# Two heads side by side in the products with values, exponentials after the copies of transposes, and the norms' small products in four groups of the TensorE array

## What is computed

```python
def rms_norm(x, g):
    y = xf * lax.rsqrt(jnp.mean(xf * xf, axis=-1, keepdims=True) + EPS)
    return (y * g.astype(jnp.float32)).astype(x.dtype)

# neighbourhood attention: local keys with a bias, and context keys
s = jnp.concatenate([s_loc + bias, s_ctx], axis=-1)
p = jax.nn.softmax(s, axis=-1)
a = p_loc @ v_loc + p_ctx @ v_ctx            # 8 heads of 64

# multi-head latent attention
q = rms_norm(cq) @ w_uq ; kn = rms_norm(rms_norm(ckv) @ w_uk)
s = qn @ kn + rope(qr) @ rope(kr)            # 64 + 32 features a head
m = softmax(s * QK_DIM ** -0.5) @ v          # 8 heads of 64

# PEER: rows of two tables of 16384 x 1024 are gathered per token
act = gelu(einsum('thkd,td->thk', exp_u[idx], hb))
out = einsum('thk,thkd->td', gate * act, exp_v[idx])
```

## Time and profile before

| what | value |
|---|---|
| median of three runs | 5595.64 us (5584.25 to 5604.5) |
| the profiled execution, its own time | 5615.22 us |
| its span, first to last instruction | 5613.4 us |
| PE busy | 4447.6 us, 79% |
| DVE busy | 3051.5 us, 54% |
| POOL busy | 2763.0 us, 49% |
| ACT busy | 1241.3 us, 22% |
| mean granted TensorE clock | 0.867 of full speed |

### The profile page before, as it was taken

The page is one execution under the profiler, slowest core; times in us unless marked ns, Lnnn a source line. Parts: engine busy times, 40 slices in busy tenths (PEclk is TensorE's granted clock), DMA queues, the critical chain, the costliest instruction groups (busy, mean ns, idle before and its releaser), DMA issues.

```text
span 5613.4 us, 57357 instructions
## 1 busy us (share of the span) xinstructions
PE 4447.6 (79%) x19168; PEld 2455.9 (44%) x19168; DVE 3051.5 (54%) x8176; ACT 1241.3 (22%) x3643; POOL 2763.0 (49%) x2566
## 2 busy tenths in 40 slices
PE   7989798889997887997855558999788889655555
PEld 4467643433585344653411115558533455311111
DVE  0211767776217776556676542431677655777643
ACT  1321222333212321112211112540133211111111
POOL 0000466666304655666677770000366466777776
PEclk9889898888998888998977888999888999877778
DMA  5544799988747878999999992114688799999999
GB/s 189 189 153 142 282 367 340 335 311 331 253 137 279 324 286 304 379 398 358 356 390 369 394 389 83 55 39 154 221 310 318 278 366 399 391 391 391 362 403 353
DMA packets 464130, 1651.73 MB, mean 294 GB/s; under 512 B 51168, under 2 KB 57440, under 8 KB 463840
## 3 DMA queue, kind: packets, MB, share of 16 engines
q0 software_dynamic: 368640, 1342.34, 63.2%
q1 hardware_dynamic: 95200, 305.73, 15.2%
HBM read 1645.77 MB, written 2.10 MB: 294 GB/s over the span
## 4 chain that ended last, share of the span: by engine, by line
PE 50%; POOL 15%; DVE 13%; DMA 11%; issue 7%; ACT 3%; SPq 0%; DVEq 0%; POOLq 0%; ACTq 0%; PEldq 0%
PE banks L647 16%; PE banks L925 10%; DMA vb<-in_peer_v_dram,idx 8%; POOL vb L1446 8%; POOL ub L1435 7%; DVE ub L1386 5%; PE banks L736 4%; PE banks L663 3%; PE banks L773 3%; PE banks L835 3%; PE banks L812 2%; PE banks L758 2%; PE banks L823 1%; DMA ub<-in_peer_u_dram,idx 1%; PE banks L715 1%
## 5 line engine op out<-in xcount | busy, mean ns | idle before, releaser
L1435 POOL DMA_INDIRECT ub<-in_peer_u_dram,idx x1280 | 1424.1, 1113 | 2270.7 <-DVE idx L1374 1375.1
L925 PE MATMUL banks<-vb,dg 128*64 128x512 f32 x5120 | 1571.7, 741 | 695.7 <-DMA vb<-in_peer_v_dram,idx 626.4
L1386 DVE CUSTOM_DVE_ANT_0 ub<-ub,h2cur 128x1024 f32<-128x1024 f32 x1280 | 1529.6, 1223 | 611.1 <-DMA ub<-in_peer_u_dram,idx 485.9
L1446 POOL DMA_INDIRECT vb<-in_peer_v_dram,idx x1280 | 1338.3, 1046 | 561.0 <-issue 342.5
L925 PEld LDWEIGHTS banks<-vb,dg 128*64 128x64 f32 x5120 | 406.7, 160 | 1596.1 <-issue 1336.4
L647 PE MATMUL banks<-region,wring 128*128 128x256 f32 x3840 | 882.2, 390 | 35.8 <-ACT region L989 25.3
L647 PEld LDWEIGHTS banks<-region,wring 128*128 128x128 f32 x3840 | 738.7, 195 | 215.8 <-issue 104.9
L1135 ACT ACTIVATE dg<-consts,wgt 128x64 f32<-128x64 f32 x1280 | 358.4, 337 | 836.5 <-PE banks L925 425.3
L647 PE MATMUL banks<-h2T,wring 128*128 128x256 f32 x1280 | 316.9, 406 | 21.1 <-ACT h2T L989 21.1
L1329 DVE SCALAR_TENSOR_TENSOR region<-region,banks 128x256 f32<-128x256 f32 x120 | 50.5, 421 | 486.0 <-PE banks L647 485.9
L736 PE MATMUL banks<-region,wring 128*128 128x256 f32 (+1 forms) x1056 | 260.7, 404 | 48.0 <-ACT region L989 48.0
(11 more groups left out here) (146 smaller groups left out, 4004.9 us busy)
## 6 DMA issues: line engine op xcount, KB each, us to landing
wring<-w_gate_dram SPq DMA_DIRECT2D x120, 512.0 KB, 5.0
wring<-w_mod_dram SPq DMA_DIRECT2D x96, 512.0 KB, 4.6
wring<-w_pq_dram SPq DMA_DIRECT2D x80, 512.0 KB, 5.4
wring<-w_branch_dram SPq DMA_DIRECT2D x60, 512.0 KB, 3.6
wring<-w_out_dram SPq DMA_DIRECT2D x40, 512.0 KB, 4.7
ub<-in_peer_u_dram,idx POOLq DMA_INDIRECT x1280, 6.6
vb<-in_peer_v_dram,idx POOLq DMA_INDIRECT x1280, 6.6
region<-in_na_rpb_dram SPq DMA_DIRECT2D x64, 256.0 KB, 3.0
```

The lines of the kernel that those rows point to most:

```text
L925: ins = nc.tensor.matmul(bank(ACC[a])[64 * g:64 * g + 64, :], dg[:, n % DG_RING, :], vb[:, n % V_RING, a * 512:(a + 1) * 512], start=first ...
L1386: nc.vector.tensor_tensor_reduce(out=ub[:, n % U_RING, :], in0=ub[:, n % U_RING, :], in1=h2cur[:, g, :], scale=1.0, scalar=0.0, op0=ALU.mu ...
L1435: pool.indirect_dma_start(ub[:, n % U_RING, :], None, u_rows, bass.IndirectOffsetOnAxis(ap=idx[:, u % IDX_RING, j:j + 1], axis=0)).then_in ...
L1446: pool.indirect_dma_start(vb[:, n % V_RING, :], None, v_rows, bass.IndirectOffsetOnAxis(ap=idx[:, u % IDX_RING, j:j + 1], axis=0)).then_in ...
```

## The change

1. `mixv` works on two units at a time: the products of units i and i+1 alternate, one in columns 0 to 63 of the array and one in columns 64 to 127, into one bank; ACT copies both with one instruction of 128 partitions.
2. On ACT the exponentials are a step of their own (`exp`), behind the copies of the transposes. They read the bank always: the biased scores are now written back into their bank by DVE, and that bank is emptied by the exponential, not by DVE. `pr` has two buffers instead of three and `ptr` three instead of two.
3. `stat` is issued for four items together. Item i uses column group i mod 4 of 32 columns; `rs` has 128 rows, and the spread of an item contracts the 32 rows of its group. `sq` has 8 buffers.

```diff
@@ run_batch @@
+            done = 0
             for i, it in enumerate(items):
...
+                if it["key"][2:] == ("cq", 1):
+                    it["group"] = items[i - 1]["group"]
+                else:
+                    it["group"] = i % 4
                 emit(("raw", l, name, i), cost)
-                if i:
-                    emit(("stat", l, name, i - 1))
-            emit(("stat", l, name, len(items) - 1))
+                if i - done == 4:
+                    emit(("stat", l, name, done, i))
+                    done = i
+            emit(("stat", l, name, done, len(items)))
@@ run_units @@
-                if 3 <= i:
-                    emit(("mixv", l, s, kind, i - 3))
+                if i < n:
+                    emit(("exp", l, s, kind, i))
+                if i >= 4 and i % 2 == 0:
+                    emit(("mixv", l, s, kind, i - 4))
@@ PE, stat @@
+                    for i in range(i0, i1):
+                        it, g = items[i], groups[i]
+                        which, q0, q1 = it["pick"][0]
+                        off = which - it["row"]
+                        ins = nc.tensor.matmul(bank(cnt["held"])[32 * g:32 * g + 32, 0:N], sel[q0:q1, off:off + 32],
+                                               sq[q0:q1, i % 8, :], start=(i == groups.index(g)),
+                                               stop=(g not in groups[i + 1:]), tile_position=(q0, 32 * g), skip_group_check=True)
@@ PE, spread @@
+                    g0 = 32 * it["group"]
                     for p0, p1, row in it["spread"]:
-                        ins = nc.tensor.matmul(bk[p0:p1, 0:N], ident[0:32, row:row + 1].broadcast_to([32, p1 - p0]),
-                                               rs[0:32, :], start=True, stop=True, tile_position=(0, p0))
+                        ins = nc.tensor.matmul(bk[p0:p1, 0:N], ident[g0:g0 + 32, g0 + row:g0 + row + 1].broadcast_to([32, p1 - p0]),
+                                               rs[g0:g0 + 32, :], start=True, stop=True, tile_position=(g0, p0))
@@ PE, mixv @@
-                    for j, vv in enumerate(un["v"]):
-                        ins = nc.tensor.matmul(bk[un["po"]:un["po"] + 64, 0:P], vv, ptr[:, i % 2, j * P:(j + 1) * P],
-                                               start=(j == 0), stop=(j == nv - 1))
+                    for j in range(nv):
+                        for e, un in enumerate(two):
+                            ins = nc.tensor.matmul(bk[64 * e:64 * e + 64, 0:P], un["v"][j],
+                                                   ptr[:, (i + e) % 3, j * P:(j + 1) * P],
+                                                   start=(j == 0), stop=(j == nv - 1), tile_position=(0, 64 * e),
+                                                   skip_group_check=True)
@@ DVE, biased score @@
-                        frees(nc.vector.tensor_tensor_reduce(out=pr[:, i % 3, 0:512], in0=bk, in1=bias[:, nb % 2, :], scale=-1.0,
...
-                        emptied(dve, key)
-                        dve.sem_inc(neg_max, 1)
+                        nc.vector.tensor_tensor_reduce(out=bk, in0=bk, in1=bias[:, nb % 2, :], scale=-1.0, scalar=st[:, 0:1],
+                                                       op0=ALU.add, op1=ALU.min, accum_out=st[:, 2:3]).then_inc(neg_max, 1)
```

More of the change, by code:

```diff
@@ L434, in na_stage @@
                         un = dict(key=(l, s, "na", t, h), q=naq[s][rows, ch, t * P:(t + 1) * P], po=p0,
-                                  dest=aT[s][rows, ch, t * P:(t + 1) * P], bias=None)
+                                  dest=aT[s][:, ch, t * P:(t + 1) * P], bias=None)
                         if s:
@@ L750, in _ @@
                 elif op == "stat":
-                    _, l, name, i = step
+                    _, l, name, i0, i1 = step
                     items = batches[(l, name)]
-                    it = items[i]
-                    cnt["sq"] += 1
+                    groups = [it["group"] for it in items]
+                    cnt["sq"] += i1 - i0
                     pe.wait_ge(sq_ready, cnt["sq"])
-                    which, q0, q1 = it["pick"][0]
-                    off = which - it["row"]
-                    ins = nc.tensor.matmul(bank(cnt["held"])[0:32, 0:N], sel[q0:q1, off:off + 32],
-                                           sq[q0:q1, i % 3, :], start=(i == 0), stop=(i == len(items) - 1),
-                                           skip_group_check=True)
-                    if i == len(items) - 1:
+                    for i in range(i0, i1):
[5 more added lines that the diff above has]
+                                               stop=(g not in groups[i + 1:]), tile_position=(q0, 32 * g), skip_group_check=True)
+                    if i1 == len(items):
                         fills(ins, (l, name, "stat"))
@@ L1007, in _ @@
                     last_spread[0] = batches[(l, name)][-1]["key"] + ("spread",)
-                    frees(nc.scalar.activation(rs[0:32, :], bk[0:32, 0:N], ACT.Sqrt, bias=epsc[0:32, 0:1]), key)
+                    rows = 32 * (max(it["group"] for it in batches[(l, name)]) + 1)
+                    frees(nc.scalar.activation(rs[0:rows, :], bk[0:rows, 0:N], ACT.Sqrt, bias=epsc[0:rows, 0:1]), key)
                 elif op == "values":
@@ L1035, in _ @@
                     st = stats[:, i % 4, :]
-                    if i >= 3:
-                        whole(act, t_hist[-1])
                     off = 0
                     for a, (_, w) in enumerate(un["k"]):
-                        dst = pr[:, i % 3, off:off + w]
                         key = un["key"] + ("s", a)
-                        if a == 0 and un["bias"] is not None:
-                            nc.scalar.activation(dst, dst, ACT.Exp, bias=st[:, 2:3], scale=-1.0, accum_out=st[:, 4:5])
-                        else:
-                            bk = whole(act, key)
-                            ins = nc.scalar.activation(dst, bk[:, 0:w], ACT.Exp, bias=st[:, 2:3], accum_out=st[:, 4 + a:5 + a])
-                            frees(ins, key)
+                        bk = whole(act, key)
+                        sign = -1.0 if a == 0 and un["bias"] is not None else 1.0
+                        frees(nc.scalar.activation(pr[:, i % 2, off:off + w], bk[:, 0:w], ACT.Exp, bias=st[:, 2:3], scale=sign,
+                                                   accum_out=st[:, 4 + a:5 + a]), key)
                         off += w
@@ L1237, in _ @@
                     emptied(dve, (l, name, "stat"))
-                    link(nc.vector.reciprocal(rs[0:32, :], rs[0:32, :]))
+                    rows = 32 * (max(it["group"] for it in batches[(l, name)]) + 1)
+                    link(nc.vector.reciprocal(rs[0:rows, :], rs[0:rows, :]))
                     dve.sem_inc(rs_ready, 1)
```

47 lines of the change are left out of this document (17 added, 30 removed).

## The result

The changed kernel takes 5535.24 us (median of 4 runs, 5523.83 to 5558.92), the kernel before, run beside it, 5600.07 us (5584.25 to 5610.14). The ratio is 0.9884, 95% interval 0.9855 to 0.9913: 65 us faster. The forecast was 148 us, so 83 us of it did not come.

What follows compares the result with a forecast made beforehand. PE bounds stretches without background; with background DMA sets the pace, in `mla_stage` PE partly too. Savings of 73 us without and 75 with background make 148 us: median 5595.6 to 5448 us, range 5370 to 5540.

Steps and rivals of the forecast that it cites:

- A pair of units: Products with values: two column groups run at once, 24 instructions cost what 12 did, 0.73 us PE work saved per unit.
- A period of two units: PE-bound `na_stage`: two units take some 6.8 us instead of 7.49, with about 0.6 us wait in every second unit.
- The 0.21 us per item: Norms' stats: cost by the skill's smaller factor instead of 0.16 us, making the sum about 8 us smaller over 210 items.
- keys of mla: Norms of mla's keys: ACT becomes the bound at 0.73 us per item, so only 0.38 us is saved.
- The spreads of eleven keys: Spreads of mla's keys: four row groups overlap, DVE takes an item in 0.43 us instead of 0.87, saving 0.43 us each.
- the 73 us forecast without background: Stages without background: CTX 29 us, norms of B 5, `na_stage` 11 and `mla_stage` of A 28 in the second layer.
- The first: Attention with background: a 2.5 us sum between most units covers the bank wait, so 0.73 us is all PE work saved.
- Norms of A and B and `na_stage`: First layer, 658 to 1185 us: PE saves 37 us, but DMA sets the pace; a quarter, 9 us, is saved.
- The last rival: Slower, by the held bank: PE waits for the whole chain every unit, 3.2 us over 96 units, 5755 us; chance 0.06.
- The second: Three `mla_stage`s with background: 60% of 34 to 35 us PE saving each, taken as 20, 22 and 22 us.
- The background keeps its pace: Rival: gathers' latency sets stages with background; only others gain, 56 us without row-group overlap, 5540 us; chance 0.16 with clock.
- Its kin, the clock: Rival: clock in emptier stages falls from 0.87 to 0.80, taking back most of 75 us; chance 0.16 shared with background.

Runs made afterwards that it cites:

- with one group: Changed kernel with all items in one column group: stats still four together but one behind the other, spreads in one row group; 5816.67 us, 0.9984 of the kernel before.
- norms alone: Kernel before with only the change's stats and spreads, attention as before; 5763.95 us (0.9896), again 5778.14 (0.99), on the chip of four kernels 5791.94 (0.9936).
- pairs in turn: Changed kernel with the two units of a pair one behind the other instead of side by side; 5580.51 us, 0.9963 of the kernel before.
- the change with late background: Changed kernel with the background step behind the exponential instead of behind the score; 5718.32, 5717.27 and 5724.45 us, ratios 0.9813, 0.9802, 0.9813 to the kernel before.
- norms alone with late background: Kernel before with only the norms' part, background step behind the transposes instead of the score; 5518.91 us (0.9856), on another chip 5747.31 (0.9846).

## Why the prediction was off

**Where there is no background, it held.** `na_stage` 119 us (forecast 118), `mla_stage` of A 130 against 128. A pair of units runs its 24 instructions in the time that 12 took, 1.53 and 1.52 us (the earlier trace rows before):

```profile
3441.23 0.88 PE L834 MATMUL banks<-consts,region 128*128 128x128 f32 x6
3442.03 1.53 PE L847 MATMUL banks<-region 128*64 128x128 f32 x24
3443.57 1.55 PE L823 MATMUL banks<-region 64*128 64x512 f32 x4
3445.06 0.88 PE L834 MATMUL banks<-consts,region 128*128 128x128 f32 x6
3445.87 1.12 PE L823 MATMUL banks<-region 64*128 64x512 f32 x2
3447.41 0.70 PE L823 MATMUL banks<-region 64*128 64x256 f32 x2 [0.42 <-ACT region L1056]
```

A period of two units is 6.8 us, as written, with the wait for the second bank in every second unit (0.42 us here, forecast 0.6). There is some luck in it: the working's own terms, 7.49 less 1.45 and plus 0.6, give 6.64 us. A wait costs more than its idle time, since the score that it splits takes 2.17 us instead of 1.49. Four stats take 0.64 us (one had taken 0.62):

```profile
59.51 18.57 PE L744 MATMUL banks<-region,wring 128*128 128x256 f32 x76
78.01 0.64 PE L768 MATMUL banks<-region,consts 128*32 128x256 f32 x8
```

In one group eight take 1.91 us, as shown above; less the drain of 0.2 us that the prediction took, four column groups give nearly four times here, an estimate. The Trainium skill, "TensorE: Matmul & The Clock Gate", Part 3, has 3.07 times for four row groups and 2.38 for three column groups, both with 512 columns moving; no run here has that form. The 0.21 us per item that was worked out from its 3.07 did not come: 0.64 us are 0.16 each. (Its 0.05 us more over 210 items are 10 us, not the 8 written.) For the pairs the factor is less, 2.39 us in turn against 1.54 (above).

For keys of mla ACT is the bound as forecast: four squares start within 2.93 us, 0.73 us each. The spreads of eleven keys fell from 9.64 us to

```profile
3564.00 5.50 PE L784 MATMUL banks<-region,consts 32*64 32x256 f32 x22
```

and with one group they were back at 9.64 us, so row groups do overlap. DVE is the bound: in the first 2.3 us of these it still works on queries, then it takes the eleven in 3.73 us without a wait, 0.34 us each (forecast 0.43). Of the 73 us forecast without background, 57 came. Of the 16 missing 12 are CTX's (17 of 29), and 10 of those its `na_stage`, which was to gain 5 us and grew by 6 at a granted clock of 0.78 (before 0.86).

**Where there is background, two steps failed.** The first is the sentence "In a stage with background a sum stands between most units and covers this wait, so there the 0.73 us is all PE work saved". The chain from score to free bank was priced from a unit without background, at 2.3 to 3.0 us; with background, ACT's stream has the background's own work between, which waits for DVE, and in the case shown the chain is 12.5 us. A sum is 2.5 us (3.65 us for the two there) and covers only part. Norms of A and B and `na_stage`: forecast 9 us saved, measured 17 lost; the norms gained 6 and `na_stage` lost 23. PE's waits for exponentials there are 42 us, and they go (4.9 us) when the background step stands behind the exponential. The lower clock is the rest of what the runs show: PE was busy as long as before with less to do. The last rival named this mechanism ("with DVE's dots in front where there is background"), but put its price on all 96 units; it struck 18 times in the 32 units of `na_stage`, 42 us, and was dismissed by the same cover.

The second is the size of the term of the three `mla_stage`s: 64 us forecast, 38 measured. With A, 18 of 20 came; with B, 10 of 22 twice. I had taken 60% of the 34 to 35 us of PE (that is 20 to 21 us, not the 22 in the sum). In B PE's busy time fell by 27 us and the stage by 10, so 16 to 17 us of waiting were new. The same step is in it, as the waits of PE in A and in B of both layers say, where before no score waited for an exponential:

```profile
PE banks L823 <- ACT region L1056: 5.9, 8, 1.4
...
PE banks L823 <- ACT region L1056: 8.8, 7, 2.5
...
PE banks L823 <- ACT region L1056: 9.5, 7, 3.4
```

The rest of the new waiting was not traced. The DMA share rose nearly as I said, to 0.91, 0.89 and 0.89, but the bytes of a stage are fixed: 22 us off B's 290 ask for 341 GB/s where 315 were, and it reached 327.

Together: 16 us are missing without background, 26 in norms of A and B and `na_stage`, 26 in the `mla_stage`s; 9 came on top in norms of the second layer with their waits, and 3 in the merges and the end. That makes the 91 us between the profiled executions. The medians are 65 us apart, because the profiled execution of before lay 15 us above its median and that of after 11 below.

**The rivals.** "The background keeps its pace" was nearer the time, 5540 us worked out, 5535 measured, by luck: it let row groups not overlap, which they do, and transfers in `mla_stage` did speed up. Its kin, the clock, took part (0.90 to 0.83 in `na_stage`). It isn't only a consequence of the waits for exponentials, since it stays at 0.84 where they are gone; PE is then the emptier engine (218 us busy of 288, norms alone 234 of 294 at 0.88), which fits that rival, and no run isolates it. That side-by-side groups slow PE is excluded by pairs in turn.

**Open.** Why the late background helps norms alone by 45 us (B's `mla_stage` in the second layer by 5, `na_stage` by 5, others by little each): there a sum stands between transposes and products, and covers their copies, instead of between scores and transposes. That is plausible and was not isolated. And what sets the clock in `na_stage` of CTX, below: whether the new attention costs up to 20 us there in about half of its executions was not tested, and it would lie in every median of a kernel that has it.

## What to carry to other kernels

When a bank's release moves to another engine, read that engine's whole stream between the write and the release, in the busiest stage and not in the clean one: whatever is queued there now holds the bank. A filler step inserted in all engines' streams covers PE and lengthens such a chain at once; put it behind the release, and try its place before rebuilding the work around it. Where a stage has a fixed number of bytes, turn the forecast into the GB/s that it asks for, and look whether the slices of before reach it.

## What the runs showed of the hardware

- **The clock of one stage differs between executions of one kernel.** `na_stage` of CTX, PE busy 93 to 96%, first and second run of the change with late background on like chips:

```profile
141.00:225.00 84.00, 81.03 (x486) 42.73 (x488) 20.40 (x88) 23.65 (x74) 0.00 (x0) 0.56 0.65 217
```

```profile
141.00:206.00 65.00, 60.31 (x499) 32.25 (x501) 20.37 (x87) 23.54 (x75) 0.00 (x0) 0.82 0.80 286
```

  The granted clock is near its lower level (1.2 GHz of 2.4) for most of the first, at the same work. Over all profiles the old attention had 0.77 to 0.87 there (7 of them), the new 0.56 to 0.83 (11, of which 6 at 0.68 or less; pairs in turn is one of them): up to 20 us that are in some executions and not in others. With the new attention it is more often there; that it comes from the attention is not shown.
- **Chips gather at different paces.** From the last `mla_stage` of the second layer to the end, mostly background alone, the kernels took 1259 to 1267 us at 369 to 372 GB/s on one kind of chip and 1324 to 1346 at 348 to 354 on the other. That is some 70 of the 230 us between 5600 and 5832; where the rest lies in the kernel before was not profiled, but in the changed one `na_stage` and A's and B's `mla_stage`s are longer too (309 against 299 us, 265 against 233, 300 against 280). The change had 0.9884 on the one kind and 0.9937 on the other, with intervals that touch; norms alone with late background had 0.9856 and 0.9846, so a smaller gain on slower chips is not shown.
- **A bank as destination costs DVE little.** The biased maximum writes PSUM in 759 ns, SBUF in 751; the read of its accumulator takes 143 ns instead of 83.
